# Who issues the small transfers: turned squares moved from the queue of weights to ScalarE

## What is computed

```
def swiglu(x, w_gate, w_up, w_down):
    return (jax.nn.silu(x @ w_gate) * (x @ w_up)) @ w_down
...
x = x + 0.5 * swiglu(rms_norm(x, ffn1_norm[layer]), ...)
x = x + mixer(rms_norm(x, mix_norm[layer]), ...)
x = x + 0.5 * swiglu(rms_norm(x, ffn2_norm[layer]), ...)
```

## Time and profile before

| | |
|---|---|
| time, median of 3 runs | 2636.38 us (2634.23 to 2637.41) |
| the profiled execution | 2630.94 us |
| its span, first to last instruction | 2629.1 us |
| mean granted TensorE clock | 0.992 of full speed |
| busy: PE / DVE / ACT / POOL | 97% / 73% / 45% / 5% of the span |
| transfers of squares | 480 issues of 16 to 64 KB, all by SP |

### The profile page before, as it was taken

How to read it: one execution, slowest core, us unless ns; L and a number is a source line. 1 busy time by engine, 2 the same in 40 slices (tenths; PEclk the granted TensorE clock), 3 DMA queues, 4 the chain that set the end, 5 groups by cost and what they waited for, 6 DMA issues and landing times.

```text
span 2629.1 us, 31692 instructions
## 1 busy us (share of the span) xinstructions
PE 2553.9 (97%) x11743; PEld 2116.6 (81%) x11743; DVE 1928.6 (73%) x2371; ACT 1173.5 (45%) x1611; POOL 136.5 (5%) x133
## 2 busy tenths in 40 slices
PE   8999999999999999999999999999999999999998
PEld 6788888877878887788888877888787888877787
DVE  7898358888983498854556988449985479798843
ACT  6445226664443444432225544335444337644431
POOL 0000004500000000000000000000000044100000
PEclk9999999999999999999999999999999999999999
DMA  5553332134533345433333454243533321244422
GB/s 178 132 144 85 95 89 79 33 121 128 136 92 94 119 108 141 112 97 97 96 96 114 116 144 111 87 134 98 150 94 107 96 87 41 88 114 136 116 89 81
DMA packets 448761, 280.92 MB, mean 107 GB/s; under 512 B 235744, under 2 KB 383968, under 8 KB 448608
## 3 DMA queue, kind: packets, MB, share of 16 engines
q1 hardware_dynamic: 448608, 278.89, 37.0%
HBM read 248.68 MB, written 2.10 MB: 95 GB/s over the span
## 4 chain that ended last, share of the span: by engine, by line
PE 70%; DVE 14%; SPq 6%; issue 5%; ACT 3%; DMA 2%; DVEq 0%; POOLq 0%; POOL 0%; ACTq 0%
PE pair L556 23%; PE pair L558 22%; PE pair L560 22%; SPq L2536 5%; DVE wl L1614 5%; ACT wh L1146 1%; DMA raw<-in_ffn_w_up 1%; DMA raw<-in_ffn_w_down 1%; DVE part L1601 1%; DVE H L1717 1%; DVE U L1624 1%; PE pair L780 1%; DVE raw L1601 1%; DVE H L1627 1%; DVE squares L1717 1%
## 5 line engine op out<-in xcount | busy, mean ns | idle before, releaser
L1614 DVE TENSOR_TENSOR wl<-raw,wh 128x1024 fp32r<-128x1024 f32 (+2 forms) x547 | 647.0, 1188 | 445.0 <-ACT wh L1146 442.4
L1146 ACT ACTIVATE wh<-raw 128x1024 fp32r<-128x1024 f32 (+2 forms) x547 | 562.7, 1030 | 823.5 <-PE pair L560 749.0
L556 PE MATMUL pair<-Hh,wl 128*128 128x512 f32 (+1 forms) x1061 | 413.6, 390 | 16.7 <-DVE Hl L1624 15.7
L558 PE MATMUL pair<-Hl,wh 128*128 128x512 f32 (+1 forms) x1061 | 414.6, 391 | 0.0
L560 PE MATMUL pair<-Hh,wh 128*128 128x512 f32 (+1 forms) x1061 | 412.2, 388 | 0.0
L556 PE MATMUL pair<-wh,Sl 128*128 128x512 f32 x960 | 379.4, 395 | 25.7 <-DVE H L1624 17.7
L556 PE MATMUL pair<-wh,Xl 128*128 128x512 f32 (+2 forms) x976 | 376.3, 386 | 16.6 <-DVE wl L1614 7.0
L558 PE MATMUL pair<-wl,Sh 128*128 128x512 f32 x960 | 377.3, 393 | 0.0
L560 PE MATMUL pair<-wh,Sh 128*128 128x512 f32 x960 | 377.0, 393 | 0.0
L558 PE MATMUL pair<-wl,Xh 128*128 128x512 f32 (+2 forms) x976 | 374.1, 383 | 0.0
L560 PE MATMUL pair<-wh,Xh 128*128 128x512 f32 (+2 forms) x976 | 374.0, 383 | 0.0
(11 more groups left out here) (325 smaller groups left out, 3287.5 us busy)
## 6 DMA issues: line engine op xcount, KB each, us to landing
raw<-in_ffn_w_gate SPq DMA_DIRECT2D x120, 512.0 KB, 4.9
raw<-in_ffn_w_up SPq DMA_DIRECT2D x120, 512.0 KB, 4.3
raw<-in_ffn_w_down SPq DMA_DIRECT2D x114, 512.0 KB, 3.5
H<-H SPq DMA_DIRECT2D x288, 64.0 KB, 2.1
raw<-in_c_w_in SPq DMA_DIRECT2D x24, 512.0 KB, 3.8
H<-squares SPq DMA_DIRECT2D x96, 64.0 KB, 2.1
raw<-in_w_in SPq DMA_DIRECT2D x10, 512.0 KB, 3.9
raw<-in_a_w_in SPq DMA_DIRECT2D x8, 512.0 KB, 3.8
```

The source lines that it names most:

```text
L556: e.matmul(o, ll, rh, start=start, stop=False, skip_group_check=again)
L558: e.matmul(o, lh, rl, start=False, stop=False, skip_group_check=again)
L1146: e.activation(part_of(n, wh), source_of(n), ACT.Copy).then_inc(whi.up(("w", n)), 1)
L1614: e.tensor_tensor(part_of(n, wl), source_of(n), part_of(n, wh).bitcast(F), ALU.subtract).then_inc(wlo.up(("w", n)), 1)
```

## The change

ScalarE issues the transfers of turned squares, four behind the `wh` of each of four units: for m = 0, 1, 2 in steps u = 3 to 6 of the groups 1, 2, 3; for m = 3 in u = 7 to 10 of group 4; for m = 4 in u = 10 to 13 of group 4. SP issues loads of weights alone (and the first inputs and the output). VectorE turns the last columns (m = 4) in u = 9 of group 4, no longer in u = 4 of group 1, into a buffer of their own that lies over `acc`; so two waits of VectorE for m = 4 go. `plan` now returns `group_loads`, which nothing reads.

```
+        squares4 = nc.alloc_sbuf_tensor_at("squares4", [128, 2, 4, 128], F, offset=acc_at)
...
 def scalar_program(e, w):
...
+            def move_blocks(s, m, part):
+                w.wait_ge(dve, ("squares", s, m))
+                for dst, src in list(block_moves(s, m))[4 * part:4 * part + 4]:
+                    e.dma_start(dst, src).then_inc(turned_in[m].sem, 16)
+                    turned_in[m].n += 16
+                turned_in[m].also(("turned", s, m))
...
                         use()
...
+                        if 3 <= u <= 6 and 0 < g < 4:
+                            move_blocks(s, g - 1, u - 3)
+                        if 7 <= u <= 10 and g == 4:
+                            move_blocks(s, 3, u - 7)
+                        if 10 <= u <= 13 and g == 4:
+                            move_blocks(s, 4, u - 10)
                         if u == 10:
                             silu_late(s, g)
...
 def vector_program(e, w):
...
             def turn_squares(s, m, *ks):
                 w.wait_ge(dve, ("h", s, m))
-                if m == 1:
-                    w.wait_ge(turned_in[4], ("turned", s, 4))
...
-                            for m in {2: (0,), 3: (1, 4), 4: (2,)}.get(g, ()):
+                            for m in {2: (0,), 3: (1,), 4: (2,)}.get(g, ()):
...
-                        if u == 4 and g == 1:
+                        if u == 9 and g == 4:
                             turn_rest_squares(s, f - GROUPED)
...
 def sync_program(e, w):
...
-            for n in range(13, len(loads) + 1):
-                for _, s, q in sorted(moves_before.get(n, ())):
-                    move_blocks(s, q)
-                if n < len(loads):
-                    fetch(n)
+            for n in range(13, len(loads)):
+                fetch(n)
```

More of the change, by code:

```diff
@@ L164, in plan @@
     loads, units, release = [], [], []
-    begins = {}
+    group_loads = {}
     holder, ring = {}, {}
@@ L188, in plan @@
         s, first, blocks = c
-        begins.setdefault(s, []).append(u)
+        group_loads.setdefault(s, []).append(len(loads))
         if first and s in AFTER_MIXER:
@@ L208, in plan @@
                 unit(512, 2, range(N_RING), 3, source, total)
-    return loads, units, release, sums, begins
+    return loads, units, release, sums, group_loads
 def weight_stream(a):
@@ L291, in build @@
         sq = [sb(f"sq{i}", [128, T], F) for i in range(2)]
+        acc_at = -(-(place[0] - 128) // 256) * 256 + 128
         acc = [sb(f"acc{i}", [128, T], F) for i in range(2)]
@@ L310, in build @@
         ident = col("ident", 0, 128)
-        loads, units, release, sums_before, begins = plan(weight_stream(a))
+        loads, units, release, sums_before, group_loads = plan(weight_stream(a))
         stage_at = -(-(stage_base - 128) // 256) * 256 + 128
@@ L338, in build, with squares @@
         squares3 = at("squares3", [128, 4, 4, 128], F, 45056 + 16384)
-        def squares(q):
-            return squares3[:, :, :, :] if q == 3 else H[:, 4 * q + 8:4 * q + 12, :, :]
+        squares4 = nc.alloc_sbuf_tensor_at("squares4", [128, 2, 4, 128], F, offset=acc_at)
+        def squares(m):
+            return {3: squares3, 4: squares4}[m][:, :, :, :] if m > 2 else H[:, 4 * m + 8:4 * m + 12, :, :]
         def block_moves(s, m):
@@ L352, in block_moves @@
                         whole = (FFN[s][0] - GROUPED - j.start + 127) // 128
-                        yield H[j, 20:20 + whole, :, i], H[i, 14:14 + whole, :, j]
+                        yield H[j, 20:20 + whole, :, i], squares4[i, 0:whole, :, j]
         def Hh(k):
@@ L1130, in scalar_program @@
             act.n = whi.n = 0
+            for event in turned_in:
+                event.n = 0
             split, used, squares = [0], [0], [0]
@@ L1721, in turn_rest_squares @@
                 w.wait_ge(dve, ("h", s, 5))
-                for k, cols in ((14, 128), (15, n - 128)):
-                    at0 = 128 * (k - 14)
-                    e.transpose(H[:, k, :, 0:cols], Hrest[:, :, at0:at0 + cols]).then_inc(dve.up(("squares", s, 4)), 1)
+                for k, cols in ((0, 128), (1, n - 128)):
+                    e.transpose(squares4[:, k, :, 0:cols], Hrest[:, :, 128 * k:128 * k + cols]).then_inc(
+                        dve.up(("squares", s, 4)), 1)
             def gate(s, g, first):
@@ L2515, in sync_program @@
         def sync_program(e, w):
-            for event in (*raw_in, *x_in, *turned_in, par_in, gain_in, out_in):
+            for event in (*raw_in, *x_in, par_in, gain_in, out_in):
                 event.n = 0
@@ L2531, in fetch @@
                 raw_in[r].also(("w", n))
[L2533 to L2546, removed]
             def load_x(t):
```

## The result

| | before | changed |
|---|---|---|
| median of 4 runs | 2635.31 us (2633.07 to 2637.41) | 2744.68 us (2743.75 to 2744.84) |
| ratio, 95% interval | | 1.0414 [1.0396, 1.0432] |
| the profiled execution, its span | 2630.94, 2629.1 us | 2744.84, 2743.1 us |
| mean granted TensorE clock | 0.992 | 0.978 |

The account below looks back on a forecast made before the run. TensorE, 97% busy, was taken as the bound, with VectorE close behind (1.3 us to spare a group). Losses 73 + 50 less 38 gained gave 85 us more: 2720 us, range for 8 in 10 2605 to 2790.

Parts of the forecast that it names:

- An issue costs ScalarE what it costs SP: On ScalarE's queue: 0.68 us an issue, as for SP's same transfers, so 2.7 us for four.
- They overlap an ACTIVATE, and the next `wh` waits for them: On ScalarE: issues hidden beside the earlier ACTIVATE, the next `wh` queued behind four; period 2.75 us.
- The prediction's own last sentence: Prediction wrong if ScalarE's issues last under 0.5 us, or if a `wh` can start beside them.
- The groups: Groups 1 to 3: late `wh` idle VectorE; 2.1 us lost in the first, 5.0 in each other, 73 us in six parts.
- The second wait that I named, at the twelfth unit: Groups 1 to 3: TensorE waits for `wl` at the eighth unit and again at the twelfth, in each of 18 groups.
- The down product: Before the first `Hh`: 32 issues take 21.8 us; 5.9 plus 2.4 us, 8.3 a part, 50 us in six.
- What SP's relief gives: Group 2's load and the down product: waits for weights queued behind SP's issues lose their cause, 38 us gained.
- Sum: 38 us: TensorE's waits saved: 17.7 us at group 2's load, 15.7 and about 1 at the down product, 3.6 for `wl`.
- Cheap issues: On ScalarE: an issue costs 0.37 us, giving 2606 us, or 2598 at no price; chance 0.19.
- Not beside an ACTIVATE: On ScalarE: issues cannot overlap an ACTIVATE, each period is 3.8 us, giving 2792 us; chance 0.13.
- SP not relieved: SP's loads late for another reason (buffers not free), the 38 us stay: about 2759 us; chance 0.03.
- The rival drawn from that sentence: Moving issues to ScalarE: the 38 us gain and the price would both be small; no chance given.

Follow-up runs that it names:

- experiment 1: Changed kernel with ScalarE's issues of m = 0, 1, 2 three steps later, in steps 6 to 9 of groups 1 to 3: 2652.4 us, ratio 1.0078.
- experiment 2: Kernel before, SP issuing all, plus ScalarE's wait for the turned squares at step 3 of groups 1 to 3: 2632.42 us, ratio 1.0003.
- experiment 3: Changed kernel with two issues behind each of eight units (steps 3 to 10) for m = 0, 1, 2: 2640.61 us, ratio 1.0035.
- experiment 4: Kernel before with m = 0, 1, 2 issued by ScalarE as in the change, m = 3, 4 still by SP: 2714.08 us, ratio 1.0315.
- experiment 5: Changed kernel with ScalarE's 16 issues of m = 4 moved into the down product: 2696.31 us, ratio 1.0237.
- experiment 10: Kernel before with only m = 4 moved: turned in group 4, issued by SP behind five down loads: 2598.52 us, ratio 0.9872.
- experiment 11: Kernel before with only m = 3 moved behind the first three down loads in SP's order: 2617.78 us, ratio 0.9947.
- experiment 6: Changed kernel with two issues behind each of eight units for m = 0 to 2 and m = 4 in the down product: 2590.11 us, ratio 0.9832.
- experiment 8: SP issues all; m = 4 turned in group 4, m = 3 sent behind three down loads, m = 4 behind two more: 2581.33 us, ratio 0.98 to before.
- experiment 9: Changed kernel with three issues behind each of steps 3 to 7 and one behind step 8, for m = 0 to 2: 2684.68 us, ratio 1.02.

## Why the prediction was right, and where it was small

**An issue costs ScalarE what it costs SP.** Right: 0.65 and 0.63 us median. With gaps and a few long ones four take 2.66 to 2.89 us in this group 2, 2.7 in the prediction. Advanced Engine Details and Errata of the Trainium skill (Clock Domains) gives both sequencers one clock; the two prices agree with that, though they don't show that the clock sets them.

**They overlap an ACTIVATE, and the next `wh` waits for them.** Right, by the starts at 1058.29 and 1058.31. The prediction's own last sentence ("or if a `wh` can start beside them") also holds: none does.

**The groups.** Right in mechanism, shown by experiments 1 to 4: VectorE idles 6.24 us where 6.3 were worked out. Undersized: I had 2.1, 5.0 and 5.0 us a part; the windows give (252.3 - 228.5) / 6 = 4.0, 6.5 and 6.2, or 16.7 us against 12.1 (a group 2 or 3 lasts 44.6 or 44.3 us by the mean, where about 43 was forecast). Two terms make up the 4.6 us. The first is the clock: I priced a wait of TensorE at its length. In group 2 of s = 4 the unit behind the wait lasts 1063.28 - 1058.02 = 5.26 us in place of 2.72. In six parts 46 matmuls of the groups 2 and 42 of the groups 3 start 0.40 to 0.46 us behind the one before, at 0.20 us too much each: 9.1 and 8.4 us, 1.5 and 1.4 a part. Without them the two groups lose 5.0 and 4.8 us. The second is group 1, in which no matmul ran at half clock: I gave VectorE a lead there and followed only the fourth delayed `wl`, but it has no such lead at the eighth unit, the first that is late, and TensorE waits at once, 1.70 us in s = 4, and again at the ninth. The second wait that I named, at the twelfth unit, is small, at most 0.7 us by the starts, and in group 2 of s = 4 it isn't there.

**The down product.** Right in mechanism, shown by experiment 5. In s = 4 the first of the 32 issues starts 1146.87 - 1123.35 = 23.5 us into group 4, 2.65 us later than before (I took 2.4); the 32 take to 1169.5, 22.6 us or 0.71 each (I took 21.8 and 0.68); `Hh` and `Hl` 1.5 us (1.4). That is 9.6 us against 8.3, and the mean of the six parts is 9.6 too. What the sum left out here is again the clock: the first units of the down product, in six 8.5 us longer than before.

**What SP's relief gives.** The step "Sum: 38 us" is mis-sized: 51 us by experiments 10 and 11. Rows 2 gave what TensorE waited; what it lost after each wait at half clock stands in no row of waits. It was in the trace before: group 2 took 33.1 us too much in six parts, of which I counted 21.3, and 40 of its matmuls at half clock are 8.0 of the rest. The other 3.8 us are the difference between my count and the gaps between the starts of matmuls, which hold 25 us in this group; 0.9 us more stand at the down product (17.6 against 16.7).

**The sum.** 73 + 50 - 38 = 85 was forecast; 100 + 58 - 51 = 107 is what the windows hold, and with the first units of the down product it is about the 114 us between the two spans. The errors had opposite signs: by the windows the losses were 35 us too small and the gain 13, which took a third of the 35 back. That the sum is nearer than its terms is luck. The clock has a part in both: over the whole program 84 matmuls start 0.40 to 0.46 us behind the one before in the trace of before, 158 in that of after, and the 74 more are 15 us. The gaps between starts of over 0.5 us, less 0.23 for the matmul itself, grew from 71 to 162 us. 91 + 15 = 106; some 5 us more are gaps of 0.3 to 0.4 us, 256 where there were 200.

**The rivals.** Cheap issues: refuted by the rows of line 1220. Not beside an ACTIVATE: refuted by the two starts. SP not relieved: refuted by the waits for weights, gone in the changed kernel, and by experiments 6, 8, 10 and 11. DMA: Bandwidth & Descriptors of the Trainium skill (Issuing engines are not separate DMA queues) says that the time of issue, all that another issuing engine saves, is "usually small relative to the DMA itself". One issue here is a fifth to a third of its transfer (0.63 to 0.65 us, and 2.1 to 3.3 until it has landed). The rival drawn from that sentence, small gain and small price, did not hold, since sixteen such issues stand in one line: where 480 x 0.65 us of them stand decides between -2.0% and +4.1%.

Left open: why 23 of ScalarE's 480 issues last over 1 us, up to 2.38, and what GpSimd does between its issues.

## What to carry to other kernels

An engine's busy share doesn't tell whether it can take a burst of issues; ask what is queued behind the burst, who needs it, and how much idle time that engine can bear within one group. Here the price fell away when the issuing engine's own period (issues plus dispatch) came down to about the consumer's work in it, two issues a unit; the better cure was to order the queue that has them already: urgent loads ahead of a burst of small transfers gave 2.0%, more than any move to another engine. And where TensorE stalls for microseconds, take the stall's price from the length of the stretch and of the unit behind it, not from the row of waits, since the slow clock behind it counts as busy.

## What the runs showed of the hardware beside this

- After the stall of 3.27 us TensorE ran at granted clock 0.50 (matmuls 0.43 us apart, not 0.23) for the 12 matmuls of a unit, and so it did after the 9.22 us in front of the down product. After the stalls of 1.70 us in group 1 and of 2.10 us in experiment 9 it did not: the matmuls behind them start 0.23 us apart, but for the first, which takes 0.31.
- GpSimd's issue of the same transfer is a row of 0.65 us, but for m = 0 to 3 one begins only every 2.4 to 4.4 us in most rows of the timeline, while for m = 4 two or three follow each other before a pause; ScalarE's and SP's follow each other at 0.67 to 0.71.
- The same transfers landed 2.7 and 3.3 us after the issue from ScalarE's queue, by the median of the page, and after 2.1 us from SP's. No row of waits names them, and the cause was not tried.
